# Interleaving the projection slabs of the second block's attention, with a buffer of its own for the compressed weights

## The chip, the cores and the metric

The kernel runs on one core of a Trainium2 chip. The metric is the device time of one execution in microseconds (us), as the median of several runs. The engines are TensorE (PE, matrix products), VectorE (DVE), ScalarE (ACT), GpSimd (POOL) and SyncE (SP, which here only issues the loads). Each engine works through its own list of instructions in order and waits on semaphores that the others raise.

## The reference, cut to what matters

Two layers of a first block come first; the change touches none of them. The second block then computes, for 512 tokens of width 1024:

```python
hn = rms_norm(h, attn_pre_norm)
proj = hn @ w_in                                   # one product, cut into the parts below
(q_n, k_c, v_c, k_s, v_s, k_w, v_w, g_n, q_w, k_sw, v_sw) = jnp.split(proj, IN_SPLITS, axis=-1)
qn = rope(q_n); k_c, k_s, k_w = rope(k_c), rope(k_s), rope(k_w)
ckv = compress(stack([k_c, v_c]), cmp_pos, cmp_w1, cmp_w2)    # gelu(blocks @ w1) @ w2, for keys and for values
o_cmp, p_cmp = compressed_attention(qn, ckv[0], ckv[1], t)
o_slc = selected_attention(qn, k_s, v_s, idx, t)              # 8 blocks of 64, 16 are chosen: all of them
o_win = banded_attention(qn, k_w, v_w, 512, None)
gates = sigmoid(g_n)
o_nsa = gates[0] * o_cmp + gates[1] * o_slc + gates[2] * o_win
o_swa = banded_attention(rope(q_w), rope(k_sw), v_sw, 128, swa_sinks)
mixed = concat(rms_norm(o_nsa), rms_norm(o_swa)) @ w_out
```

after which come a residual, a feed-forward part and the output.

## The kernel before, in words

All weights come in **slabs** of 128 x 1024 floats. SP loads a slab into one of four slots (`raw`), ACT copies it to `w_hi` (line 1099, function `split`), DVE subtracts to get the remainder `w_lo` (line 1510), and PE multiplies: each product is three matmuls, high by high, high by low and low by high (`mm3`, lines 534 to 536). `w_hi` and `w_lo` have two halves (`SPL = 2`), used in turn: slab n may be split when PE is through with slab n - 2 (semaphore `slab_used`), and a slot can be loaded again when DVE has split its slab (`lo_ready`).

The attention part of the second block has 25 slabs, which before come in three runs:

- 13 **t slabs** (`T_ORDER`, lines 792 to 812): the values to be compressed, then the keys kc, ks, kw, kx, then four slabs of queries qn and four of sliding queries qx. PE makes 24 matmuls of 512 columns for each. ACT copies the bank out (line 1372) and copies it once more with halves swapped (line 1374, four instructions); DVE rotates (function `rope`, lines 1825 to 1840: two products and one sum, or four half sums for ks, kw, kx).
- 4 **v slabs** (lines 815 to 824): values and gates, 24 matmuls of 408 columns each. ACT then copies the values out (`v2`, lines 1394 and 1395) and takes exponentials of the gates.
- 8 **c slabs** (function `cmp_hidden`): the weights `cmp_w1`, four for keys and four for values, each only 12 matmuls of 256 columns. Their other operand are the blocks `xe_hi`, `xe_lo`, which DVE builds out of the rotated keys and the raw values (functions `blocks` and `blocks_low`) with one ACT copy between (line 1388).

Then a chain of small steps makes the compressed branch: a gelu (line 1402), two transposes (842), copies (1406), the second weights (856, 861), copies (1408, 1410), 64 score matmuls of 31 columns (875), mask, maximum and difference on DVE (1883 to 1891, `cmp_front`), exponentials on ACT (1414), sums and coefficients on DVE (1899 to 1910, `cmp_back`), 32 transposes (886) and copies of them (1432). The attention proper goes over a list of units (`UNITS`), as a pipeline: scores (903 and 909), maximum (1943), exponential (1426), scaling (1959), transposes (922), copies (1444), products with the values (943). The first two units' scores stand before the 32 transposes, the others behind.

The order on each engine is written out by hand: each of the blocks for SP, PE, ACT and DVE has its own loop over the slabs, and the step that belongs to slab i is put into the loop by a condition on i.

## Time and profile before

| | |
|---|---|
| time, median of 3 runs | 1905.05 us (1902.78 to 1906.3) |
| the profiled execution: span, first to last instruction | 1903.6 us |
| PE busy | 1829.9 us, 96% of the span |
| DVE, ACT, POOL busy | 1333.0, 973.8, 190.6 us |
| mean granted clock of PE | 0.985 |
| slabs of the second block's attention part, in that execution | 1199.4 to 1312 us |
| small steps of the compressed branch | 1312 to 1336.8 us |

The page gives no time of the profiled execution other than its span; what lies around the span is not in it. The span stands 1.45 us under the median of the runs and inside their range. The times in the rows below count from the span's start. A granted clock of 1.00 is the upper of TensorE's two levels (2.4 GHz), 0.50 the lower (1.2 GHz).

### The profile page before, as it was taken

What the parts mean: (1) busy time and instruction counts of PE and PEld (TensorE: products, weight loads), DVE (VectorE), ACT (ScalarE), POOL (GpSimd) and SP (SyncE); (2) the same over time, 40 slices, a digit from 0 to 9 for tenths busy, and PEclk for the clock granted to TensorE, in tenths of its full rate; (3) what the DMA queues carried; (4) which work ended last, traced back from release to release, by engine and by line L of the source; (5) the groups of instructions that cost most, each with busy time, mean ns of one, the idle gap of its engine ahead of it and who ended that gap; (6) DMA issues with size and microseconds to landing.
All of it is one profiled execution on the core that took longest, in us unless ns stands there. A gap on an engine that the chain in (4) does not pass through costs nothing.

```text
span 1903.6 us, 27030 instructions
## 1 busy us (share of the span) xinstructions
PE 1829.9 (96%) x8975; PEld 1456.3 (77%) x8975; DVE 1333.0 (70%) x1885; ACT 973.8 (51%) x1550; POOL 190.6 (10%) x135
## 2 busy tenths in 40 slices
PE   6999999999999999999999999997998999999998
PEld 5775778888888875678888888886656678888887
DVE  6989677777655899767777655694666477777544
ACT  5569654444433468764444443674655554444322
POOL 0100120000133100120000033100012300000111
PEclk9999999999999999999999999997999999999999
DMA  6220233333234330133333233434000223332332
GB/s 172 68 77 1 67 93 95 99 99 93 77 98 117 84 81 12 34 94 95 99 99 94 76 100 97 107 85 132 1 1 2 88 71 94 99 99 84 86 98 75
DMA packets 285095, 154.46 MB, mean 81 GB/s; under 512 B 16949, under 2 KB 283095, under 8 KB 285015
## 3 DMA queue, kind: packets, MB, share of 16 engines
q1 hardware_dynamic: 284596, 153.26, 27.9%
q8 instruction: 45, 0.74, 0.2%
q14 instruction: 35, 0.29, 0.0%
q10 hardware_dynamic: 419, 0.17, 0.0%
HBM read 151.31 MB, written 2.10 MB: 81 GB/s over the span
## 4 chain that ended last, share of the span: by engine, by line
PE 78%; DVE 10%; issue 6%; ACT 5%; DMA 0%; DVEq 0%; SPq 0%; ACTq 0%
PE bank L534 24%; PE bank L536 23%; PE bank L535 23%; DVE cacc L1647 3%; PE bank L903 1%; DVE w_lo L1510 1%; PE bank L943 1%; DVE nmax L1714 1%; PE bank L922 1%; ACT w_hi L1099 1%; DVE pr L1959 1%; DVE nmax L1943 1%; PE bank L1018 0%; DMA x_in<-in_x 0%; PE bank L683 0%
## 5 line engine op out<-in xcount | busy, mean ns | idle before, releaser
L1099 ACT ACTIVATE w_hi<-raw 128x1024 fp32r<-128x1024 f32 (+1 forms) x337 | 336.2, 1004 | 511.9 <-PE bank L536 507.4
L1510 DVE TENSOR_TENSOR w_lo<-raw,w_hi 128x1024 fp32r<-128x1024 f32 (+1 forms) x337 | 404.0, 1204 | 256.2 <-ACT w_hi L1099 255.3
L534 PE MATMUL bank<-h_hi,w_hi 128*128 128x512 f32 x1448 | 569.6, 393 | 10.9 <-DVE w_lo L1510 10.7
L535 PE MATMUL bank<-h_lo,w_hi 128*128 128x512 f32 x1448 | 564.5, 390 | 0.0
L536 PE MATMUL bank<-h_hi,w_lo 128*128 128x512 f32 x1448 | 564.4, 390 | 0.0
L534 PEld LDWEIGHTS bank<-h_hi,w_hi 128*128 128x128 f32 x1448 | 272.5, 188 | 75.2 <-issue 11.9
L535 PEld LDWEIGHTS bank<-h_lo,w_hi 128*128 128x128 f32 x1448 | 272.3, 188 | 58.3 <-issue 2.2
L536 PEld LDWEIGHTS bank<-h_hi,w_lo 128*128 128x128 f32 x1448 | 272.4, 188 | 56.6
L534 PE MATMUL bank<-a_hi,w_hi 128*128 128x512 f32 x528 | 206.1, 390 | 0.0
L536 PE MATMUL bank<-a_hi,w_lo 128*128 128x512 f32 x528 | 205.5, 389 | 0.0
L535 PE MATMUL bank<-a_lo,w_hi 128*128 128x512 f32 x528 | 205.4, 389 | 0.0
L1647 DVE SCALAR_TENSOR_TENSOR cacc<-u_pad,lc,cacc 128x512 f32<-128x512 f32 x240 | 179.5, 793 | 1.6
L1595 DVE TENSOR_TENSOR zr<-bank,rstd 128x512 f32<-128x512 f32 x132 | 90.8, 688 | 80.5 <-PE bank L536 68.4
L1601 DVE SCALAR_TENSOR_TENSOR tz<-zr,lc,tz 128x511 f32<-128x511 f32 x176 | 131.9, 750 | 19.9 <-DVE tz L1601 6.8
L1168 ACT ACTIVATE a_hi<-tz 128x512 f32 (+1 forms) x66 | 41.8, 633 | 160.6 <-DVE tz L1609 160.6
L536 PEld LDWEIGHTS bank<-a_hi,w_lo 128*128 128x128 f32 x528 | 99.1, 188 | 20.8
L534 PEld LDWEIGHTS bank<-a_hi,w_hi 128*128 128x128 f32 x528 | 99.1, 188 | 20.5
L535 PEld LDWEIGHTS bank<-a_lo,w_hi 128*128 128x128 f32 x528 | 99.1, 188 | 20.2
L2027 POOL TENSOR_TENSOR sq<-x 128x512 f32 (+1 forms) x16 | 29.3, 1832 | 636.6 <-DVE x L1790 636.6
L1611 DVE TENSOR_TENSOR a_lo<-tz,a_hi 128x512 f32 x66 | 45.7, 693 | 61.5 <-ACT a_hi L1168 61.5
L1164 ACT ACTIVATE tz<-zr,lc 128x512 f32<-128x512 f32 x88 | 71.1, 808 | 31.4 <-DVE zr L1595 31.4
L1601 DVE SCALAR_TENSOR_TENSOR tz<-zr,cols,tz 128x510 f32<-128x510 f32 x88 | 65.9, 749 | 9.4 <-DVE tz L1601 1.7
(313 smaller groups left out, 2217.9 us busy)
## 6 DMA issues: line engine op xcount, KB each, us to landing
raw<-in_w_up SPq DMA_DIRECT2D x132, 512.0 KB, 3.7
raw<-in_w_in SPq DMA_DIRECT2D x39, 512.0 KB, 3.9
raw<-in_w_down SPq DMA_DIRECT2D x48, 384.0 KB, 3.1
raw<-in_w_down SPq DMA_DIRECT2D x48, 320.0 KB, 2.9
raw<-in_w_o SPq DMA_DIRECT2D x16, 512.0 KB, 3.4
raw<-in_cmp_w SPq DMA_DIRECT2D x8, 512.0 KB, 4.0
raw<-in_w_out SPq DMA_DIRECT2D x8, 512.0 KB, 4.3
raw<-in_w_uq SPq DMA_DIRECT2D x8, 288.0 KB, 2.9
```

Source lines behind the costliest of these rows:

```text
L534: mm(o, wh, mh, start=start, stop=False)
L535: mm(o, wh, ml, start=False, stop=False)
L536: return mm(o, wl, mh, start=False, stop=stop)
L1099: last = A_(dst(w_hi), src(raw), ACT.Copy)
L1164: A_(tz[:, s, :], zr[:, s % 2, :], ACT.Identity, bias=c_b(ch), scale=c_w1(ch)).then_inc(z1_done.sem, 1)
L1168: A_(a_hi[:, bass.ds(i * 2 + j, 1), :], tz[:, 2 * j + 1:2 * j + 2, :], ACT.Copy).then_inc(ah_done.sem, 1)
L1510: last = v.tensor_tensor(dst(w_lo), src(raw), dst(w_hi).bitcast(f32), ALU.subtract)
L1595: v.tensor_tensor(zr[:, s % 2, :], bank[s][:, :], rstd[:, 0, :], ALU.mult).then_inc(zr_done.sem, 1)
L1601: ins = v.scalar_tensor_tensor(tz[:, s, a:b], zr[:, s % 2, a + sh:b + sh], tap(n, ch), tz[:, s, a:b], ALU.mult, ALU.add)
L1611: v.tensor_tensor(a_lo[:, bass.ds(i * 2 + j, 1), :], tz[:, 2 * j + 1:2 * j + 2, :], a_hi[:, bass.ds(i * 2 + j, 1), :].bitcast(f32), ALU.su ...
L1647: ins = v.scalar_tensor_tensor(cacc[:, c, :], src, wc, cacc[:, c, :], ALU.mult, ALU.add)
L2027: link(p.tensor_tensor(sq[:, :], chunk, chunk, ALU.mult))
```

## The change

A table `SEQ2` sets one order of the 25 slabs for all engines: v slabs go between the first t slabs, the c slabs go singly between other slabs, and the sliding queries come last. The c slabs get buffers of their own (`cw_hi`, `cw_lo`); the other slabs go on using `w_hi` and `w_lo` in turn (`ring2`), and a slab waits for the slab before it in the same buffer (`before2`). The banks are dealt out anew (`T_BANK`, `VG_B`), `swapped` becomes two buffers. The steps of the compressed branch are put between the slabs: the gelu and transposes for keys behind the fourth c slab and t6, the scores behind the last c slab, the mask and exponentials at t10, the transposes at t11. The last rotation (the fourth qx) moves into the attention pipeline's third round on DVE.

```diff
+SEQ2 = [("t", 0), ("t", 1), ("v", 0), ("t", 2), ("v", 1), ("t", 3), ("v", 2), ("c", 0), ("t", 4), ("c", 1), ("v", 3),
+        ("c", 2), ("t", 5), ("c", 3), ("t", 6), ("c", 4), ("t", 7), ("c", 5), ("t", 8), ("c", 6), ("t", 9), ("c", 7),
+        ("t", 10), ("t", 11), ("t", 12)]
+T_BANK = (0, 1, 0, 1, 0, 1, 2, 3, 0, 1, 0, 2, 3)
+def ring2(n):
+    return sum(kind != "c" for kind, _ in SEQ2[:n]) % SPL
+def before2(n):
+    same = [m for m in range(n) if (SEQ2[m][0] == "c") == (SEQ2[n][0] == "c") and (SEQ2[n][0] == "c" or ring2(m) == ring2(n))]
+    return same[-1] if same else 1
...
 # SP
+            for p, (kind, i) in enumerate(SEQ2):
+                if p == 6:
+                    sp.wait_ge(x_done.sem, x_done.at(DEPTH, 0))
...
 # PE
+            def turned_slab(p, i):
+                for j in banked_before(i):
+                    pe.wait_ge(rc_done.sem, j + 1)
+                    pe.wait_ge(sw_done.sem, j)
...
+            for p, (kind, i) in enumerate(SEQ2):
+                slab_ready(G2, p)
...
+                if (kind, i) == ("t", 3):
+                    root_columns()
+                if (kind, i) == ("t", 6):
+                    cmp_turn(0)
+                if (kind, i) == ("t", 7):
+                    cmp_keys()
+                if (kind, i) == ("c", 7):
+                    cmp_scores()
+                if (kind, i) == ("t", 10):
+                    cmp_turn(1)
+                if (kind, i) == ("t", 11):
+                    cmp_values()
+                    for n in range(2 * NT):
+                        cmp_turned(n)
...
+                if u == 1:
+                    pe.wait_ge(sw_done.sem, 12)
...
-                if s == 1:
-                    for n in range(2 * NT):
-                        cmp_turned(n)
 # ACT, split
+                if isinstance(g, int) and g == G2 and SPL <= n0 < S2_O:
...
+                    act.wait_ge(slab_used.sem, G2 * RAW + before2(n0) + 1)
+                    A_(halves2(n0)[0], raw[:, n0 % RAW, :], ACT.Copy).then_inc(hi_ready.sem, 1)
+                    return
 # ACT, loop
+            for p, (kind, i) in enumerate(SEQ2):
...
+                split(N, G2, p + SPL)
+                if (kind, i) == ("t", 10):
+                    log_exp_table()
+                    for e in range(2):
+                        act.wait_ge(cs_sub.sem, e + 1)
+                        A_(cs[:, e, :, :], cs[:, e, :, :], ACT.Exp).then_inc(cs_exp.sem, 1)
+                act.wait_ge(slab_used.sem, G2 * RAW + p + 1)
+                if kind == "t":
+                    copied(i)
...
+                if (kind, i) == ("t", 3):
+                    act.wait_ge(rcol_mm.sem, 1)
...
+                    blocks_high(0)
+                if (kind, i) == ("v", 3):
+                    values_out()
+                if (kind, i) == ("c", 2):
+                    blocks_high(1)
...
+                if (kind, i) == ("t", 10):
+                    turned_out(1)
 # DVE, loop
+            for p, (kind, i) in enumerate(SEQ2):
...
+                if p + SPL < S2_O:
+                    split(G2, p + SPL)
...
+                if p == 3:
+                    blocks(0)
+                if kind == "t" and i >= 3:
+                    rope(i - 2)
+                if (kind, i) == ("v", 2):
+                    blocks_low(0)
+                if (kind, i) == ("v", 3):
+                    blocks(1)
+                if (kind, i) == ("t", 5):
+                    blocks_low(1)
...
+                if (kind, i) == ("t", 10):
+                    cmp_front()
+                if (kind, i) == ("t", 11):
+                    cmp_back()
...
+                if s == 2:
+                    rope(len(ROPED) - 1)
```

What the tables do to the order of instructions is seen at three places. Line numbers in the lists of the change are those of the changed kernel; lines 1164 and 1171 there are ACT's slab copy (1099 before), 1606 DVE's remainder (1510 before).

**ACT, at the exponentials of the compressed scores (`cs`).** Before:

```order
L1406 ACTIVATE hid<-bank 128x62
L1408 ACTIVATE kcT<-bank 128x62 [waits kv_mm]
L1410 ACTIVATE vcn<-bank 31x128 [waits kv_mm]
L1104 ACT_TABLE_LOAD
L1414 ACTIVATE cs<-cs 128x496 [waits cs_sub] x2
L1426 ACTIVATE pr_91,rsum<-bank,nmax 128x128 [waits nm_done] x4
L1432 ACTIVATE ct_all<-bank 31x4x128 [waits ct_mm] x8
```

With the change:

```order
L1164 ACTIVATE w_hi<-raw 128x1024 [waits slab_used,raw_ready0]
L1176 ACT_TABLE_LOAD
L1480 ACTIVATE cs<-cs 128x496 [waits cs_sub] x2
L1438 ACTIVATE tz<-bank 128x512 [waits rope_done,slab_used]
L1440 ACTIVATE swapped_84<-bank 32x512 x4
L1465 ACTIVATE hid<-bank 128x62 [waits hid_t]
L1465 ACTIVATE hid<-bank 128x62
L1171 ACTIVATE w_hi<-raw 128x1024 [waits slab_used,raw_ready1]
L1438 ACTIVATE tz<-bank 128x512 [waits rope_done,slab_used]
L1440 ACTIVATE swapped_83<-bank 32x512 x4
L1510 ACTIVATE vcn<-bank 31x128 [waits kv_mm]
L1514 ACTIVATE ct_all<-bank 31x4x128 [waits ct_mm] x8
```

The exponentials stood behind all slab work; now they stand between the split of the last t slab (t12) and the copies of the banks of t10 and t11, and the copies of the values' hidden part (`hid`) stand behind them.

**DVE, at the mask and the sums of the compressed scores.** Before:

```order
L1510 TENSOR_TENSOR w_lo<-raw,w_hi 128x1024 [waits hi_ready,rope_done]
L1510 TENSOR_TENSOR w_lo<-raw,w_hi 128x1024 [waits hi_ready] x11
L1915 TENSOR_SCALAR gates<-gates 128x96 [waits gate_exp]
L1916 RECIPROCAL gates<-gates 128x96 [waits dve_link]
L1883 TENSOR_TENSOR cs<-bank,const 128x496 [waits cs_mm] x2
```

With the change:

```order
L1606 TENSOR_TENSOR w_lo<-raw,w_hi 128x1024 [waits hi_ready] x2
L1927 TENSOR_TENSOR tz<-tz,const 128x512 [waits sw_done]
L1928 TENSOR_TENSOR tz<-swapped_83,const 128x512
L1937 TENSOR_TENSOR qx<-tz 128x512 [waits dve_link]
L1946 TENSOR_TENSOR cs<-bank,const 128x496 [waits cs_mm,rope_done]
```

and, behind the rest of `cmp_front` and one scaling of x:

```order
L2017 SCALAR_TENSOR_TENSOR x<-x,cols,rstd 128x512
L1927 TENSOR_TENSOR tz<-tz,const 128x512 [waits sw_done]
L1928 TENSOR_TENSOR tz<-swapped_84,const 128x512
L1937 TENSOR_TENSOR qx<-tz 128x512 [waits dve_link]
L1962 TENSOR_REDUCE csum<-cs 128x16 [waits cs_exp,rope_done]
```

The mask addition now stands behind the remainder of t12 and a rotation, and the sums behind one more rotation, which waits for the swapped copy of t10.

**DVE, at the first blocks' remainder `xe_lo`, which the first c slab waits for.** With the change:

```order
L1606 TENSOR_TENSOR w_lo<-raw,w_hi 128x1024 [waits hi_ready]
L1606 TENSOR_TENSOR cw_lo<-raw,cw_hi 128x1024 [waits hi_ready]
L1927 TENSOR_TENSOR tz<-tz,const 128x512 [waits sw_done]
L1928 TENSOR_TENSOR tz<-swapped_84,const 128x512
L1937 TENSOR_TENSOR k_ks<-tz 64x512 [waits dve_link]
L1937 TENSOR_TENSOR k_ks<-tz 64x512 x3
L1606 TENSOR_TENSOR w_lo<-raw,w_hi 128x1024 [waits hi_ready,rope_done]
L1919 TENSOR_TENSOR xe_lo<-xe,xe_hi 128x1088 [waits xe_h]
L1606 TENSOR_TENSOR cw_lo<-raw,cw_hi 128x1024 [waits hi_ready]
```

Before, this step stood at the ninth t slab with four t slabs and all v slabs between it and the first c slab; now it stands at the last slab before that c slab.

## Rows read from the trace of the kernel before

**Rows 1.** Busy time by stage: stretch, its length, busy us (instructions) per engine, PE clock.

```profile
core 0: us, PE busy (x) PEld busy (x) DVE busy (x) ACT busy (x) POOL busy (x), PEclk, DMA share, GB/s
1273.50:1292.40 18.90, 18.30 (x98) 17.89 (x97) 11.57 (x14) 8.43 (x11) 0.00 (x0) 1.00 0.36 114
1292.40:1312.00 19.60, 14.42 (x98) 13.15 (x97) 8.77 (x8) 13.08 (x22) 0.00 (x0) 0.91 0.57 180
1312.00:1336.80 24.80, 17.45 (x125) 13.94 (x124) 11.60 (x26) 9.93 (x26) 0.00 (x0) 0.59 0.22 66
```

**Rows 2.** Waits from 1199 to 1341 us: total us, times, longest.

```profile
PE bank L534 <- DVE w_lo L1510: 6.3, 6, 2.6
```

**Rows 3.** PE in order of time, c slabs: start, us, instruction, [idle before <- releaser].

```profile
1299.34 0.39 PE L534 MATMUL bank<-w_hi,xe_hi 128*128 128x256 f32 x1 [2.57 <-DVE w_lo L1510]
...
1306.18 0.39 PE L534 MATMUL bank<-w_hi,xe_hi 128*128 128x256 f32 x1 [0.58 <-DVE w_lo L1510]
```

**Rows 4.** PE in order of time, small steps and first units.

```profile
1313.56 0.33 PE L842 MATMUL bank<-const,hidc 62*128 62x62 f32 x2 [1.23 <-ACT hidc L1402]
...
1314.42 1.06 PE L861 MATMUL bank<-w2v,hid 128*31 128x64 f32 x8
1315.84 7.04 PE L875 MATMUL bank<-kcT,qn 64*128 64x31 f32 x64 [0.36 <-ACT vcn L1410]
...
1330.02 1.92 PE L886 MATMUL bank<-const,cs 128*31 128x128 f32 x8 [5.17 <-DVE cs L1910]
...
1335.80 1.07 PE L886 MATMUL bank<-const,cs 128*31 128x128 f32 x8 [0.32 <-ACT ct_all L1432]
1336.81 0.70 PE L903 MATMUL bank<-k_ks,qn 64*128 64x256 f32 x4
...
1339.31 0.44 PE L922 MATMUL bank<-const,pr 128*128 128x128 f32 x2 [0.50 <-DVE pr L1959]
```

**Rows 5.** Busy time and PE clock in three stretches of the small steps.

```profile
1315.00:1322.60 7.60, 7.24 (x69) 7.00 (x67) 0.41 (x1) 1.55 (x2) 0.00 (x0) 0.50 0.40 128
...
1325.00:1330.00 5.00, 0.00 (x0) 0.00 (x0) 4.83 (x13) 1.90 (x6) 0.00 (x0) 0.50 0.00 0
...
1335.00:1337.00 2.00, 1.68 (x15) 1.11 (x14) 0.00 (x0) 1.63 (x4) 0.00 (x0) 1.00 0.00 0
```

**Rows 6.** ACT in order of time.

```profile
1222.95 1.06 ACT L1099 ACTIVATE w_hi<-raw 128x1024 fp32r<-128x1024 f32 x1 [1.33 <-PE bank L536]
1224.04 0.60 ACT L1372 ACTIVATE tz<-bank 128x512 f32<-128x512 f32 x1
1224.66 2.40 ACT L1374 ACTIVATE swapped<-bank 32x512 f32<-32x512 f32 x4
1228.39 1.06 ACT L1099 ACTIVATE w_hi<-raw 128x1024 fp32r<-128x1024 f32 x1 [1.33 <-PE bank L536]
...
1256.49 1.12 ACT L1388 ACTIVATE xe_hi<-xe 128x1088 fp32r<-128x1088 f32 x1
...
1326.18 1.20 ACT L1414 ACTIVATE cs<-cs 128x496 f32<-128x496 f32 x2 [9.09 <-DVE cs L1891]
```

**Rows 7.** DVE in order of time.

```profile
1224.11 1.23 DVE L1510 TENSOR_TENSOR w_lo<-raw,w_hi 128x1024 fp32r<-128x1024 f32 x1 [0.30 <-ACT w_hi L1099]
...
1232.59 2.78 DVE L1838 TENSOR_TENSOR k_kw<-tz 64x512 f32<-64x512 f32 x4
...
1244.76 0.69 DVE L1838 TENSOR_TENSOR qn<-tz 128x512 f32<-128x512 f32 x1
...
1257.71 1.29 DVE L1820 TENSOR_TENSOR xe_lo<-xe,xe_hi 128x1088 fp32r<-128x1088 f32 x1 [0.51 <-ACT xe_hi L1388]
...
1322.91 1.25 DVE L1883 TENSOR_TENSOR cs<-bank,const 128x496 f32<-128x496 f32 x2 [7.50 <-PE bank L875]
...
1327.05 1.24 DVE L1899 TENSOR_REDUCE csum<-cs 128x16 f32<-128x496 f32 x2
```

**Rows 8.** Loads on SP's queue, from the page: times issued, KB, us to landing.

```profile
raw<-in_cmp_w SPq DMA_DIRECT2D x8, 512.0 KB, 4.0
```

More of the change, by code:

```diff
@@ L278, in build @@
         STAT = bank[7]
-        VG_B = bank[4], bank[5], bank[1], bank[2]
+        VG_B = bank[4], bank[5], bank[2], bank[3]
         C_B, CT_B = (bank[4], bank[5]), (bank[6], bank[7])
@@ L807, in _, with value_slab @@
                 last.then_inc(slab_used.sem, 1)
-                if i == 5:
-                    pe.wait_ge(rr_done.sem, 1)
-                    for t in range(NT):
-                        last = mm(bank[6][:, t:t + 1], zr[0:1, 0, t * P:(t + 1) * P], ones[0:1, 0:1], start=True, stop=True)
-                    last.then_inc(rcol_mm.sem, 1)
-            pe.wait_ge(sw_done.sem, len(ROPED) - 2)
-            for i in range(KD // VG_K):
-                slab_ready(G2, S2_V + i)
-                w = parts(S2_V + i, VG_K, VG)
+            def value_slab(p, i):
+                w = parts2(p, VG_K, VG)
                 for t in range(NT):
@@ L849, in _ @@
-            pe.wait_ge(gate_exp.sem, NT)
-            cmp_turn(0)
-            cmp_turn(1)
-            pe.wait_ge(w2_ready, 48)
-            pe.wait_ge(rope_done.sem, len(ROPED))
-            pe.wait_ge(hid_done.sem, 2)
-            for m in range(2):
-                last = mm(bank[4][:, 0:2 * NC], w2k[:, m, :], hid[:, m, :], start=m == 0, stop=m == 1)
-            last.then_inc(kv_mm.sem, 1)
-            pe.wait_ge(hid_done.sem, 4)
-            for v in range(KV2):
-                for m in range(2):
-                    last = mm(bank[5][0:NC, v * HD2:(v + 1) * HD2], hid[:, 2 + m, v * NC:(v + 1) * NC], w2v[:, m, :],
-                              start=m == 0, stop=m == 1)
@@ L863, in _, with cmp_keys, cmp_values @@
-            last.then_inc(kv_mm.sem, 1)
+            def cmp_keys():
+                pe.wait_ge(w2_ready, 48)
+                pe.wait_ge(hid_done.sem, 2)
+                for m in range(2):
+                    last = mm(bank[4][:, 0:2 * NC], w2k[:, m, :], hid[:, m, :], start=m == 0, stop=m == 1)
+                last.then_inc(kv_mm.sem, 1)
+            def cmp_values():
+                pe.wait_ge(hid_done.sem, 4)
+                pe.wait_ge(sw_done.sem, 9)
+                for v in range(KV2):
+                    for m in range(2):
+                        last = mm(bank[1][0:NC, v * HD2:(v + 1) * HD2], hid[:, 2 + m, v * NC:(v + 1) * NC], w2v[:, m, :],
+                                  start=m == 0, stop=m == 1)
+                last.then_inc(kv_mm.sem, 1)
@@ new lines, in _ @@
+                if (kind, i) == ("t", 11):
+                    act.wait_ge(kv_mm.sem, 2)
+                    A_(vcn[0:NC, :], bank[1][0:NC, 0:KV2 * HD2], ACT.Copy).then_inc(kv_done.sem, 1)
+                    for n in range(2 * NT):
+                        e, t = divmod(n, NT)
+                        act.wait_ge(ct_mm.sem, n + 1)
+                        A_(ct_all[0:NC, :, t, e, :], CT_B[n % 2][0:NC, :].rearrange("p (c n) -> p c n", c=PAIRS),
+                           ACT.Copy).then_inc(ct_done.sem, 1)
@@ L1919, in evict @@
+            for n0 in range(S2_O - SPL, S2_O):
+                split(G2, n0 + SPL)
             def evict(i):
```

295 lines of the change are left out of this document (150 added, 145 removed).

## The prediction

> **What bounds the kernel now.** I read the busy time by stage first, then the waits, then PE's own order of time, and last ACT and DVE at the places that PE waits for. In the t and v slabs PE is the bound: in the v stage it is busy 18.30 of 18.90 us at full clock [rows 1]. In the c stage it is busy only 14.42 of 19.60 us at a mean clock of 0.91, and in the small steps 17.45 of 24.80 us at 0.59 [rows 1]. PE's work is the same before and after the change, and so is everything up to the first slab and after the first few attention units. So I count what PE loses between these two points, as waits and as clock, in both versions; the difference is the change of the time.
>
> **What PE loses now.** Waits: 6.3 us for slabs that DVE has not split yet [rows 2], most of it between c slabs, as the 2.57 and 0.58 us [rows 3]; 1.23 us for the gelu, 0.36 for the copies behind it, 5.17 for mask, exponentials and coefficients, 0.32 twice for copies of transposes, 0.50 at the first units [rows 4]: together 14.2 us. Clock: busy time times the missing share of the clock, 14.42 x 0.09 = 1.3 in the c stage and 17.45 x 0.41 = 7.2 in the small steps [rows 1]: 8.5 us. The sum is 22.7 us, which is also the most that any order of this work could gain.
>
> **What the change takes away.** The run of short c slabs goes, with its waits, and the steps of the compressed branch get slabs to run beside. If all of it were hidden, the 22.7 us would be gone. It is not, because each engine still takes its list in order, and some steps now stand behind others that are late.
>
> **The front, where a c slab waits for DVE.** The first c slab (c0) needs `xe_lo`. Its chain starts when PE ends t3: ACT copies the bank, 0.60 + 2.40 us, and the two small copies of the column roots (0.3, my estimate), then makes `xe_hi`, 1.12, then splits the second c slab, 1.06 [rows 6], because DVE's list has the remainder of that slab, 1.23, ahead of `xe_lo`, 1.29 [rows 7]. With three hand-offs of 0.1 (ACT's split ends at 1224.01, DVE's starts at 1224.11 [rows 6, 7]) that is 8.3 us. PE has beside it only v2, 18.30 / 4 = 4.6 [rows 1], and the column roots (1.0 us, estimated as eight matmuls like those of the small steps, which take 1.06 [rows 4]). So c0 waits some 2.7 us. The fifth c slab (c4) waits likewise. Behind the remainder of t6 DVE has a rotation of kx (two products of 0.69 and 2.78: 4.2), the values' `xe_lo` (1.29), two gate steps and one scaling of x (1.5 together, estimated from the 0.69 of one operation), and then the split of c4, 1.23 [rows 7]: 8.2 us; PE has t6, 5.44 (ACT's splits stand 5.44 apart, at 1222.95 and 1228.39 [rows 6]) and a transpose of 0.33 [rows 4]: 5.8. So c4 waits 2.4. I add 1.5 for c3, t6 and the score matmuls, where ACT's eight copies of the values and the last query rotation are a little late (two or three waits of the size of the 0.58 [rows 3]). Front: 6.6 us. It is at least 0, if ACT and DVE get ahead, and at most some 9.
>
> **The tail, where a chain goes through four lists.** At t10 ACT's list has: the split of t12, which waits for the end of t10 (the same half of `w_hi`); the exponentials, which wait for DVE's differences; then the copies of t10 and of the values' hidden part. DVE's list has the remainder of t12, a rotation, and only then mask, maximum and difference. So from the end of t10: split 1.06, remainder 1.23, rotation 3 x 0.69 = 2.1, mask to the first difference 3.3 (1322.91 to the exponentials at 1326.18), exponentials 1.20, copies 3.00, two small copies 0.5 (estimate), and some 0.1 each for six hand-offs: 13.0 us [rows 6, 7]. PE has t11 and one transpose beside it, 5.44 + 0.33 = 5.8. So PE stands still for **7.2 us** before the compressed values (line 861 of the kernel before). What is queued behind it on PE is everything, the transposes and t12 included. The next wait follows at once: DVE's rotation of t10's queries waits for the same copies, and the sums stand behind it: 2.1 + 3.0 (1327.05 to PE's first transpose at 1330.02 [rows 4, 7]) = 5.1, less the two small copies and the values' 1.06: some **3.5 us** before the transposes. These wait for their copies as before, 0.6. Behind them comes t12, 5.44, and the first unit; the second unit's bank was t12's, so it waits for ACT's split and copies, 1.06 + 3.00 + 0.3 = 4.4, less a first unit's scores of at most 0.9: **3.5 us**. Then the last rotation, 2.1, stands in DVE's list before the scaling that the first products wait for, on top of the 0.50 of before [rows 4]: 2.6, and I take 3.0, since the 32 transposes no longer cover the first pair's maximum and exponentials. Tail: 17.8 us.
>
> **The clock.** Before, the transposes behind the 5.17 us wait ran at 0.50 at first; the 32 of them took 1330.02 to 1336.81 with 0.6 of waits, 6.2, against 4 x 1.07 = 4.3 at the pace of the last eight [rows 4, 5]: 1.9 lost. They stand behind a longer gap now, so I take 1.9 again, 0.5 for the compressed values (half of 1.06), 1.3 for one of the two front gaps (the c stage's loss behind its 2.57 us gap [rows 1, 3]) and 0.7 for the second unit's start (half of what two units take). The 64 score matmuls took 7.04 us at 0.50 [rows 4, 5]; they follow a c slab now, and I take them at full clock, at no loss. Clock: 4.4 us; 0 at the least, and some 8 if every gap in front and t12 too are hit.
>
> The Trainium skill (TensorE: Matmul & The Clock Gate, section on HAM oscillation in real kernels) says that idle gaps between bursts of matmuls are what brings TensorE down to half its clock, and advises keeping bursts close together. By it the long gap of the new tail costs clock as well as time, and breaking up the run of c slabs saves clock in front; the trace agrees as to gaps, but it also has 7.24 busy us out of 7.60 at 0.50 [rows 5], which the advice alone would not give. What the rule would do if it held in the change's favour is the first rival.
>
> **Parts costed at nothing.** The loads: SP issues the same loads, the second weights of the compressed branch (three small loads) eleven slabs sooner; its wait ahead of them has been met by then. A load is issued four slabs ahead and lands in 4.0 us [rows 8]; between issue and use at least two slabs pass, one of them of 5.44, so it stays hidden; without that cover each late slab would cost up to 4.0. The bank waits of t slabs two positions apart are covered by the v and c slabs between. POOL has nothing here. ACT's and DVE's total work fits beside PE's and is unchanged but for where it stands.
>
> **The sum.** After: 6.6 + 17.8 + 4.4 = 28.8 us lost, before: 22.7. The change costs 6.1 us: 1903.6 + 6.1 = 1909.7 us for the profiled span. The median of the runs stands 1.45 above that span, so I forecast **1911 us**.
>
> **The rivals.** A measurement of this kernel can tell 0.2%, 3.8 us, from no change: 1901.2 to 1908.9 count as no difference.
> (1) The clock stays up. Then 28.8 - 4.4 = 24.4 against 22.7: 1.7 us slower, 1906.8, no difference. For it: the front's slabs are dense, and c slabs stand between long ones. Against it: the gap of 2.57 us before was followed by a stage at 0.91, and the tail's gap is longer [rows 1, 3].
> (2) DVE keeps pace in front. If `xe_hi` and the c slabs' splits get through before PE asks, the front's 6.6 and its 1.3 of clock go: 20.9, or 1.8 us faster, 1903.3, no difference. It decides from the point where c0 and c4 show no wait. Against it: the sums 8.3 against 5.6 and 8.2 against 5.8.
> (3) Faster: the exponentials are back before t10 ends. The score matmuls are done a whole t slab earlier; if DVE's mask came ahead of the remainder of t12, the chain would be over beside t10 and t11, the 7.2 and 3.5 would go and with them the 1.9 and 0.5 of clock: 15.7 lost, 7.0 us faster, **1898**. Against it: DVE's list has the remainder first, and that waits for ACT's split, which waits for the end of t10.
> That the change doesn't move what it says is no case: the order of the lists shows it.
>
> **How the numbers follow.** The forecast's case has 0.70, (1) 0.12, (2) 0.10, (3) 0.08. The forecast's own case runs from 1907 to 1918: 28.8 with the front at 4 and the clock at 3, up to the front at 9 and the clock at 8. I let the range reach down over (1) and (2), to 1903, which leaves out (3) and some of the edges. Faster is (3) and the lower edge of (2), 0.10; no difference is (1), most of (2) and the lower edge of the forecast's case, 0.26; slower is the rest, 0.64.
>
> **What would show it.** In the profile after: PE idle of about 7 us ahead of the compressed values' matmuls, released by ACT's `hid` copies; a second idle of 3 to 4 us ahead of the transposes; a third at the second unit, released by ACT's swapped copy of t12; two waits of 2 to 3 us at c0 and c4, released by DVE; ACT's exponentials idle for some 5 us for DVE's differences; half clock around the transposes. The prediction is wrong if the compressed values' matmuls follow t11 without a wait, or if PE's lost time in front is over 10 us, when the slab supply would be the bound.

## The result: 11 to 16 us slower, and more than forecast

| | before | with the change |
|---|---|---|
| median of the runs | 1903.91 us (1902.71 to 1906.3, 4 runs) | 1919.7 us (1918.1 to 1921.15, 4 runs) |
| ratio, 95% interval | | 1.0075 (1.0062 to 1.0089) |
| the same on a second occasion | 1906.87 us (10 runs) | 1917.78 us (4 runs), ratio 1.0060 (1.0044 to 1.0077) |
| profiled execution: time, span | span 1903.6 us | 1919.27 us, span 1917.2 us |
| mean granted clock | 0.985 | 0.980 |

The change costs 11 to 16 us. The forecast was 6 us, with a range up to 1918: the sign was right, the size too small. The first median lies 1.7 us above the range, that of the second occasion inside it: on which side of the range's end it falls is partly chance. The account below goes by the profile.

The waits of PE in the profile of the changed kernel, from 1199 to 1365 us (total us, times, longest):

```profile
PE bank L899 <- ACT hid L1465: 6.2, 1, 6.2
PE bank L926 <- DVE cs L1973: 3.6, 1, 3.6
PE bank L973 <- ACT swapped L1440: 3.5, 1, 3.5
PE bank L575 <- issue: 2.3, 1, 2.3
PE bank L575 <- DVE cw_lo L1606: 2.0, 1, 2.0
PE bank L992 <- DVE pr L2062: 1.6, 1, 1.6
```

The run of c slabs with its 6.3 us of waits [rows 2] is gone. In its place stand the waits that the prediction named: 6.24 us before the values' product (line 899), 3.60 before the transposes (926), 3.47 before the second unit (973), 2.25 and 1.97 at c0 and c4 (575). For c0 the profile names no releaser ("issue"), but DVE's `xe_lo`, which c0 needs, ended at 1239.09 and c0 began at 1239.19 (first line below). How the longest wait comes about is seen in DVE's and in ACT's order of time (start, us, instruction, idle before and what ended it):

```profile
1237.81 1.28 DVE L1919 TENSOR_TENSOR xe_lo<-xe,xe_hi 128x1088 fp32r<-128x1088 f32 x1
...
1307.44 1.22 DVE L1606 TENSOR_TENSOR w_lo<-raw,w_hi 128x1024 fp32r<-128x1024 f32 x1 [10.09 <-ACT w_hi L1164]
...
1310.63 1.26 DVE L1946 TENSOR_TENSOR cs<-bank,const 128x496 f32<-128x496 f32 x2
```

```profile
1313.91 1.20 ACT L1480 ACTIVATE cs<-cs 128x496 f32<-128x496 f32 x2 [5.20 <-DVE cs L1954]
1315.02 0.58 ACT L1438 ACTIVATE tz<-bank 128x512 f32<-128x512 f32 x1
```

The scores were finished at 1297.8. DVE idled 10.09 us for the high half of t12 (line 1606), and only then, behind a rotation, came to the mask (1946); ACT idled 5.20 us for DVE. So far the prediction holds. What it has wrong is in the busy time by stage of the changed kernel (columns as in rows 1; the last stretch, inside the one before it, runs from the scores of the third unit to those of the seventh):

```profile
1239.00:1293.40 54.40, 51.86 (x270) 44.91 (x270) 40.76 (x57) 36.50 (x60) 0.00 (x0) 0.97 0.47 136
1293.40:1312.20 18.80, 18.50 (x114) 15.13 (x114) 6.76 (x10) 5.37 (x7) 0.00 (x0) 0.82 0.26 84
1312.20:1335.00 22.80, 12.65 (x65) 9.18 (x65) 12.69 (x22) 12.91 (x24) 0.00 (x0) 0.78 0.07 24
1335.00:1360.40 25.40, 20.30 (x117) 10.73 (x116) 15.43 (x46) 14.50 (x43) 0.00 (x0) 0.66 0.07 22
1340.20:1354.40 14.20, 12.56 (x57) 6.17 (x56) 9.85 (x33) 6.34 (x24) 0.00 (x0) 0.50 0.02 5
```

The clock is down behind the scores (0.82) and in the first units (0.66, for 14 us 0.50). The third to the eighth unit in the kernel before:

```profile
1336.80:1350.10 13.30, 12.80 (x105) 7.11 (x104) 10.58 (x34) 9.65 (x31) 0.00 (x0) 1.00 0.01 2
```

and two lines of PE's order of time in the changed kernel, the second unit behind its wait and the fifth, whose 64x384 products took 0.92 us before:

```profile
1339.17 0.80 PE L973 MATMUL bank<-k_kw,qn 64*128 64x128 f32 x4 [3.47 <-ACT swapped L1440]
...
1346.61 1.65 PE L973 MATMUL bank<-k_ks,qn 64*128 64x384 f32 x4
```

From the third unit's start to the ninth's the kernel before took 13.3 us (1336.81 to 1350.15), the changed kernel 20.2 (1340.23 to 1360.43), the same matmuls. At the third unit the changed kernel is 3.4 us behind, at the ninth 10.3. That is the place to explain. These times count from the span's start. The first slab of this part starts anywhere from 1198.0 to 1200.9 us in the profiles below, though all kernels are the same up to there (1199.43 before, 1198.89 with the change); counted from that slab the changed kernel is 4.0 us behind at the third unit and 10.8 at the ninth. Where a text below says "from the first slab", it counts so.

Theories for the runs below: **A**, the waits are the cost, and the clock is a small term as the prediction has it; **B**, the lower clock behind these gaps was undersized; **C**, the cost sits in the front, in the interleaved c slabs. A and B don't exclude each other.

### The profile page after: what moved, and what is told of

It reads as the page before. It is cut to its first block, busy times and chain, and to the rows that moved or that the text cites. A ratio compares the mean times of both kernels' runs of the same rounds, so it can differ in the third digit from the quotient of the medians.

```text
span 1917.2 us, 27037 instructions
## 1 busy us (share of the span) xinstructions
PE 1837.7 (96%) x8975; PEld 1460.4 (76%) x8975; DVE 1333.1 (70%) x1885; ACT 973.0 (51%) x1550; POOL 191.2 (10%) x135
## 4 chain that ended last, share of the span: by engine, by line
PE 79%; DVE 9%; issue 6%; ACT 5%; DMA 0%; DVEq 0%; SPq 0%; ACTq 0%
PE bank L575 24%; PE bank L576 23%; PE bank L577 23%; DVE cacc L1746 3%; PE bank L973 2%; PE bank L1013 1%; PE bank L992 1%; DVE nmax L1813 1%; DVE w_lo L1609 1%; DVE pr L2062 1%; DVE nmax L2046 1%; ACT w_hi L1171 1%; PE bank L724 0%; DMA x_in<-in_x 0%; ACT swapped L1440 0%
## 5 line engine op out<-in xcount | busy, mean ns | idle before, releaser
L575 PE MATMUL bank<-h_hi,w_hi 128*128 128x512 f32 x1448 | 571.3, 395 | 10.9 <-DVE w_lo L1609 10.2
L1171 ACT ACTIVATE w_hi<-raw 128x1024 fp32r<-128x1024 f32 (+3 forms) x314 | 312.0, 1000 | 488.2 <-PE bank L577 483.7
L1609 DVE TENSOR_TENSOR w_lo<-raw,w_hi 128x1024 fp32r<-128x1024 f32 (+3 forms) x314 | 376.0, 1203 | 237.7 <-ACT w_hi L1171 237.1
L575 PEld LDWEIGHTS bank<-h_hi,w_hi 128*128 128x128 f32 x1448 | 273.3, 189 | 74.9 <-issue 10.6
L1527 ACT ACTIVATE pr<-bank,nmax 128x257 f32<-128x257 f32 (+5 forms) x96 | 47.3, 498 | 54.2 <-DVE nmax L2046 49.1
```

What stands on the lines that cost most here:

```text
L575: mm(o, wh, mh, start=start, stop=False)
L1171: last = A_(dst(w_hi), src(raw), ACT.Copy)
L1527: A_(pr2[:, s % 3, e, 0:n], S2_B[s % 2][e][:, c0:c0 + n], ACT.Exp, bias=nmax[:, st:st + 1], accum_out=rsum[:, st:st + 1]).then_inc(e_done. ...
L1609: last = v.tensor_tensor(dst(w_lo), src(raw), dst(w_hi).bitcast(f32), ALU.subtract)
```

## Experiments

Each run's own kernel before ran beside it on the same chip; "against before" is the difference of those two medians. Kernels of one group ran together, save where said (`fill_tail` ran with group 2, the two other runs of group 1 with group 6).

**1. The gaps filled.** Extra matmuls on PE that nobody reads stand in its waits: 24, 14 and 13 in `fill_tail`, the 13 alone in `fill_units`. `after_again` is the changed kernel itself, beside `fill_units`.

```diff
+            def fill(to, n):
+                for i in range(n):
+                    mm(to[:, :], ones_r[:, :], h_hi[:, i % KD, :], start=i == 0, stop=i == n - 1)
...
+                    fill(bank[6], 24)
                     cmp_values()
+                    fill(bank[6], 14)
                     for n in range(2 * NT):
...
+                if s == 1:
+                    fill(bank[4], 13)
                 if s < len(UNITS):
                     scores2(s)
```

> The changed kernel with 51 extra TensorE products (128x512, 0.227 us each in its rows) into a bank that nobody reads, put where its TensorE waits: 24 (5.4 us) into the wait of 6.24 us before the values' second product, 14 (3.2 us) into the 3.60 us before the transposes, 13 (3.0 us) between the first and the second unit of the attention (3.47 us). Every wait stays as long as it was, only the idle time is used. Theory A (the waits themselves are the cost, the clock is a small term, as the prediction had it): same time within 1 us, 1918 to 1921. Theory B (the lower clock that follows these gaps was undersized: 0.78 over 12.65 busy us and 0.66 over 20.30 busy us make 2.8 + 6.9 us): the granted clock from 1312 to 1360 us comes near 1.00 and the time falls by 5 to 9 us, to 1910 to 1914.

> The changed kernel itself once more, beside the others on one chip and with a second profile: 1917 to 1921, 13 to 16 us above the kernel before. In its profile the ninth unit of the attention starts within 1 us of 1360.4, as the order of the program sets it; what lies behind that (556.8 us to the end in the first profile, 553.4 in the kernel before, the same instructions) comes out between 553 and 558: if it is near 554, the 3 us there are chance, if near 557, they belong to the change.

> The changed kernel with the third of the three fills of the run fill_tail alone: 13 extra products (3.0 us) between the first and the second unit of the attention, into a bank that nobody reads. Theory B1 (the lower clock that costs is the one behind the gap between the first units, 17 us of units at half speed): 5 to 6.5 us faster than the changed kernel, as fill_tail was. Theory B2 (it begins with the gaps of 6.24 and 3.60 us further ahead, and the units only go on with it): under 2 us faster.

Measured: `fill_tail` 1913.38 us, 7.8 against before, where the changed kernel has 11 to 16 (granted clock 1.00 and 0.93 in the stretches that had 0.78 and 0.66); `after_again` 1917.78, 10.9 against before (13 to 16 expected); `fill_units` 1914.51, 7.6. The third fill alone does what the three do. The four runs of `fill_units` went from 1912.9 to 1918.4 us, those of `after_again` from 1916.6 to 1918.2: the medians alone don't separate the two, and the reading rests on the profiles. PE's order of time in `fill_units` and the busy time from its third to its eighth unit:

```profile
1334.33 3.29 PE L905 MATMUL bank<-h_hi,ones_r 128*128 128x512 f32 x13
1338.00 0.49 PE L977 MATMUL bank<-k_kw,qn 64*128 64x128 f32 x4 [0.38 <-ACT swapped L1446]
...
1344.26 0.92 PE L977 MATMUL bank<-k_ks,qn 64*128 64x384 f32 x4
```

```profile
1338.80:1354.30 15.50, 12.98 (x104) 7.15 (x104) 13.56 (x43) 9.74 (x33) 0.00 (x0) 1.00 0.03 11
```

The wait for ACT ends where it ended before, 4.2 us behind the first unit's start; PE worked in it, and the units behind run at 1.00, where the first 14 us of the changed kernel's had 0.50 (64x384 in 0.92 us, not 1.65). They take 15.5 us in place of 20.2. Theory B (form B1): 4.7 us of the change's cost is the clock behind the 3.47 us gap between the first two units. In the medians it is 3.3 us beside `after_again`, less than the 5 to 6.5 expected. In `fill_tail` the units take 17.1 us: the third and fourth run at full speed, but behind a later wait of 2.22 us the fifth is at half (1.54 us). The second profile of the changed kernel agrees with the first (20.1 us for the units, 161.5 us from the first slab to the ninth unit in both); from the ninth unit to the end it took 556.1 us, the first 556.8: in the upper half of the range expected.

**2. The chain ahead of the splits.** `chain_early` moves the mask to the differences ahead of DVE's remainder of t12, the exponentials ahead of ACT's split of t12, the sums ahead of a rotation. `chain_query_first` also puts t12 ahead of the values' product and the transposes on PE.

```diff
 # DVE
+                if (kind, i) == ("t", 10):
+                    cmp_front()
                 if p + SPL < S2_O:
                     split(G2, p + SPL)
+                if (kind, i) == ("t", 11):
+                    cmp_back()
...
 # PE and ACT, chain_query_first alone
-                if (kind, i) == ("t", 11):
+                if (kind, i) == ("t", 12):
                     cmp_values()
```

> The changed kernel with the chain of the compressed scores moved ahead in two lists: VectorE does the mask, maximum and subtraction before it waits for the high half of the last query slab (it stood idle 10.1 us there), ScalarE does the table and the exponentials before that high half, and VectorE does the sums and coefficients before the rotation. TensorE's order stays. The 6.24 us before the values' product and the 3.60 us before the transposes should go; 0 to 1.6 us may come up behind ScalarE's copy of the eleventh query (3 us) between the second and the third transposes; the 3.47 us before the second unit stays. Theory A: 8.2 to 9.8 us faster than the changed kernel, 1909.5 to 1911. Theory B: beside that, 2 to 5 us of clock, 1904 to 1908. Theory C (the cost sits in the front, in the interleaved compressed slabs, and the tail only shifts): less than 4 us faster, 1915 or more.

> As the run chain_early, and TensorE's last query slab before the values' product and the transposes, so that these cover ScalarE's 3 us of copies of it. The 3.47 us before the second unit should go; about 1 us should come up before the third transposes (ScalarE's copies 3.0 us and two smaller ones, against 1.06 + 2.1 us of TensorE's work). Theory A: 2 to 3.5 us faster than chain_early, 1906 to 1909. Theory B: 3 to 7 us faster than it, since the attention's first units no longer run behind a gap, 1898 to 1904.

Measured: `chain_early` 1911.74 us, 6.2 against before. The 6.24 us are gone, of the 3.60 are left 1.5, and 1.8 came up at the copies of the transposes: 6.5 us less waiting, and the third unit starts 7.4 us earlier from the first slab. Its units still take 20.4 us, at 0.63, for the 3.47 us gap stayed. In the medians, each against its own before, the gain on the changed kernel is 9.6 us by its first occasion and 4.8 by its second; by the profile it is theory A for these two waits, and C falls. `chain_query_first` 1905.2 us, 0.4 below before and 6.5 faster than `chain_early`: B's gain of 3 to 7, not A's of 2 to 3.5. Its rows:

```profile
1324.62 1.08 PE L926 MATMUL bank<-const,cs 128*31 128x128 f32 x8 [3.55 <-ACT ct_all L1514]
...
1331.38 0.70 PE L973 MATMUL bank<-k_ks,qn 64*128 64x256 f32 x4 [0.53 <-ACT pr L1527]
...
1335.94 0.44 PE L992 MATMUL bank<-const,pr 128*128 128x128 f32 x2 [2.35 <-DVE pr L2062]
1336.31 0.69 PE L1013 MATMUL bank<-pt,v 128*64 128x128 f32 x4
1336.93 1.65 PE L973 MATMUL bank<-k_ks,qn 64*128 64x384 f32 x4
```

The wait didn't shrink to 1 us as I expected: as much as before, 3.55 us, now stands between the transposes, since ACT copies t12's bank first. From the first slab the third unit starts 3.3 us earlier than in `chain_early` (the 3.47 us ahead of the second unit are gone, as is the 1.5 us before the transposes), and the units take 16.9 us in place of 20.4. So about half of the gain comes from fewer waits ahead of the units, and half lies in the units, which ran at 0.90 in place of 0.63: here a wait of the same length cost less ahead of the transposes than ahead of the first units.

**3. The last query out of the way.** As `chain_early`, with t12 in bank 7, which the first units don't need; ACT copies it after the sixth unit. The copies of t11 move behind those of the transposes, and the values' product behind the transposes.

```diff
-T_BANK = (0, 1, 0, 1, 0, 1, 2, 3, 0, 1, 0, 2, 3)
+T_BANK = (0, 1, 0, 1, 0, 1, 2, 3, 0, 1, 0, 2, 7)
...
 # ACT, attention loop; DVE's rotation of it moves from s == 2 to s == 8
+                if s == 5:
+                    copied(12)
```

> As the run chain_early, and the last query slab in a bank of its own (bank 7) that the first two units don't need: ScalarE copies the slab after the sixth unit, VectorE rotates it after the eighth (it is first used by the 17th unit), and the copy of the slab before it stands behind the transposes' copies. No wait of TensorE between the tenth query slab and the second unit should be over 1 us. Theory A: 3.5 to 5 us faster than chain_early, 1904.5 to 1907.5. Theory B: 5 to 9 us faster than it, 1896 to 1902, and below the kernel before (1903.9).

Measured (beside group 2): 1904.14 us, 1.5 below before (ratio 0.9992, 0.9981 to 1.0002): 7.6 us faster than `chain_early`, inside B's gain of 5 to 9, though not as low as B's 1902, since `chain_early` had come out at the upper end. Up to the third unit two waits over 1 us remain in the tail, 2.19 before the transposes (where none was expected) and 2.29 at the third unit, and the units take 18.8 us.

**4. A gap made on purpose.** On top of `last_query_later` PE waits ahead of the first unit for seven operations of POOL; then the same with 30 and with 41 extra matmuls in that wait (the last on another occasion).

```diff
 # POOL
+            for n in range(6):
+                link(p.tensor_tensor(sq[:, :], one, one, ALU.mult))
+            p.tensor_tensor(sq[:, :], one, one, ALU.mult).then_inc(gap_done, 1)
 # PE, first unit
+                    fill(bank[4], 30)
+                    pe.wait_ge(gap_done, 1)
```

> As the run last_query_later, with a wait of TensorE before the attention's first unit, made by seven steps of GpSimd that start when the last query slab is done (about 1.2 us each, 8 to 9 us in all; GpSimd does nothing else there). Theory A: slower than last_query_later by the wait less what the small waits behind it had (about 2 us), 6 to 8 us. Theory B: by the wait and 3 to 6 us of lower clock in the first units, 10 to 14 us.

> As the run gap_idle, with 30 extra products of TensorE (6.8 us) in that wait, into a bank that nobody reads. The wait's end doesn't move. Theory A: the same time as gap_idle within 1.5 us. Theory B: 4 to 7 us faster than gap_idle, since the first units run at the higher clock; 6 to 8 us slower than last_query_later.

> As gap_idle, with 41 extra products in the 9.82 us of that wait (9.8 us at the 0.239 us each that the 30 of gap_filled took), in place of the 30 that left its last 2.77 us open; into a bank that nobody reads. If the gap right ahead of the units is what lowers the clock: the products of the third to the sixth unit (64x256 and 64x384) run at 0.70 and 0.92 us, not 1.22 and 1.65, and the ninth unit starts 14 to 16 us behind the third, not 18.5; 3 to 5 us faster than gap_idle and gap_filled. If the small units lower it by themselves: half speed again, and the same 18 us.

Measured: `gap_idle` 1913.24 us, 9.1 against before; `gap_filled` 1914.93, 10.8; `gap_filled_whole` 1912.53, 7.8. `gap_idle` lies 10.6 us above `last_query_later`, each against its own before, which is the low end of B's 10 to 14; but the units of `last_query_later` were partly at half speed already, and in the profiles `gap_idle` is only 8.1 us behind it at the ninth unit, counted from the first slab. So this pair doesn't tell A from B. In `gap_idle` the units right behind the gap ran at half speed at once:

```profile
1336.64 0.80 PE L978 MATMUL bank<-k_ks,qn 64*128 64x128 f32 x4 [9.82 <-issue]
...
1338.94 1.22 PE L978 MATMUL bank<-k_ks,qn 64*128 64x256 f32 x4
```

The first fill was too short, as PE's order of time in `gap_filled` shows:

```profile
1326.33 7.16 PE L908 MATMUL bank<-h_hi,ones_r 128*128 128x512 f32 x30
1336.26 0.49 PE L983 MATMUL bank<-k_ks,qn 64*128 64x128 f32 x4 [2.77 <-POOL sq L2233]
1336.90 0.49 PE L983 MATMUL bank<-k_kw,qn 64*128 64x128 f32 x4
1338.20 1.23 PE L983 MATMUL bank<-k_ks,qn 64*128 64x256 f32 x4 [0.59 <-ACT pr L1540]
```

and in `gap_filled_whole`:

```profile
1326.56 9.73 PE L908 MATMUL bank<-h_hi,ones_r 128*128 128x512 f32 x41
1336.51 0.49 PE L983 MATMUL bank<-k_ks,qn 64*128 64x128 f32 x4 [0.23 <-POOL sq L2233]
1337.15 0.49 PE L983 MATMUL bank<-k_kw,qn 64*128 64x128 f32 x4
1338.45 0.70 PE L983 MATMUL bank<-k_ks,qn 64*128 64x256 f32 x4 [0.59 <-ACT pr L1540]
```

With 2.77 us left open the first two units still ran at full speed (0.49 us) and the third at half (1.23 us), with 0.23 us the third at full speed too (0.70); but for the length of the fill nothing in these rows differs. So here the gap right ahead lowers the clock, not the small units by themselves. The price is less than I expected. The busy time from the third to the eighth unit, `gap_idle` and `gap_filled_whole`:

```profile
1338.90:1357.30 18.40, 16.22 (x104) 8.79 (x104) 12.78 (x42) 13.98 (x41) 0.00 (x0) 0.78 0.01 1
1338.40:1355.00 16.60, 14.11 (x104) 7.90 (x104) 12.44 (x40) 13.87 (x41) 0.00 (x0) 0.93 0.01 1
```

That is 1.8 us where 3 to 5 were expected, since a later gap in these units, 2.1 us ahead of one unit's transposes, is followed by half speed in all three. The medians, 1.4 us apart against their own before, lie within each other's intervals and show nothing by themselves.

**5. Small products between large ones.** As `last_query_later`, with the scores spread over the eight steps of t10 and the transposes over those of t12; then also c0's and c4's waits taken away on DVE.

```diff
+                    if i == 10:
+                        cmp_scores(k)
+                    if i == 12:
+                        cmp_turned(k)
 # DVE, between_and_front alone
+                if (kind, i) == ("v", 2):
+                    blocks_low(0)
                 if p + SPL < S2_O:
                     split(G2, p + SPL)
+                if (kind, i) == ("c", 3):
+                    gate_sums()
```

> As the run last_query_later, and the small products put between the large ones: of the 64 score products (4.13 us in one piece in the profile of the changed kernel) eight behind every third of... each of the eight steps of the tenth query slab, and of the 64 transposes (8 us in one piece) eight behind each of the eight steps of the last query slab. No work is added or left out. Theory B (what follows a stretch of small products runs at the lower clock: the query slab behind the scores ran 0.63 us a product for 5.7 us, where 0.39 is usual): the granted clock of 1293 to 1312 us rises from 0.82 to 0.95 or more and that of the transposes' stretch too, 3 to 6 us faster than last_query_later, 1898 to 1901. Theory A (waits only): no wait is removed but up to 2 us before the transposes, 1902 to 1904.

> As the run between, and two steps of VectorE in the front in another order: the low half of the first blocks before the split that waits for ScalarE (2.25 us before the first compressed slab), the gates' sums and the final gain behind the split of the next compressed slab (1.97 us before the fifth). Both waits should shrink to under 1 us: 2.5 to 3.5 us faster than the run between by the waits, and some 1 us more by the clock (0.97 over 51.86 busy us in this stretch).

Measured (beside `gap_idle`): 1912.09 us, 8.0 against before, and 1906.9, 2.8. The first is a miss. The clock did rise: t10 and the scores took 11.5 us together at a granted clock of 1.00, where `last_query_later` took 12.5 at 0.73. But the order made new waits behind ACT, 3.0 us for the bank of t12 and 5.1 for the first exponentials. The second differs by the front alone: its two waits fell to 0.2 and 0.5 us (0.9 came up elsewhere), and from the first slab the first unit starts 3.6 us earlier.

**6. The versions that beat both.** `later_and_front` is `last_query_later` with the front of group 5. `later_front_sums` also puts the sums right behind the differences on DVE and the splits of the first two output slabs into the attention.

```diff
 # DVE
                 if (kind, i) == ("t", 10):
                     cmp_front()
+                    cmp_back()
...
-            for n0 in range(S2_O - SPL, S2_O):
-                split(G2, n0 + SPL)
...
+                if 6 <= s < 6 + SPL:
+                    split(G2, S2_O + s - 6)
```

> As the run last_query_later, with VectorE's two steps in the front in the other order (those of between_and_front: the low half of the blocks ahead of a split, the gates' sums and the final gain behind one), and the small products in one piece again. Theory A: 2.5 to 3.5 us faster than last_query_later by the two waits (2.25 and 1.97 us) alone. Theory B: 3 to 5. Either way below the kernel before, by 3.5 to 6 us. If it is not faster than last_query_later, the waits of the front were paid for elsewhere.

> As the run later_and_front, with VectorE's sums and coefficients right behind the exponentials (it idled 5.6 us there) and the splits of the first two slabs behind the attention moved into the attention (2.4 us of VectorE and 1.1 of ScalarE stood between the last query slab and the first unit's maximum). The 2.19 us before the transposes and most of the 2.29 us before the third unit should go: 3 to 5 us faster than later_and_front, 6 to 10 us faster than the kernel before.

Measured (beside `fill_units`): 1898.61 us, 8.3 below before, ratio 0.9956 (0.9942 to 0.9969); and 1895.37, 11.5 below before, ratio 0.9946 (0.9932 to 0.9961). Both gains are somewhat larger than expected (3.5 to 6 and 6 to 10). The second version is faster than both kernels. Its largest waits of PE up to 1420 us, and the attention's first units, in order of time:

```profile
PE bank L995 <- DVE pr L2078: 4.6, 6, 1.0
PE bank L995 <- ACT pt L1546: 2.1, 1, 2.1
PE bank L928 <- ACT ct_all L1518: 1.5, 3, 0.9
```

```profile
1318.59 0.49 PE L976 MATMUL bank<-k_ks,qn 64*128 64x128 f32 x4
...
1320.52 0.70 PE L976 MATMUL bank<-k_ks,qn 64*128 64x256 f32 x4 [0.59 <-ACT pr L1534]
...
1323.76 0.92 PE L976 MATMUL bank<-k_ks,qn 64*128 64x384 f32 x4
```

From the first slab the third unit starts 19.5 us earlier than in the changed kernel and 15.6 earlier than in the kernel before.

**7. What the change's own two parts are worth.** From `later_front_sums`: the c slabs back in the common buffers, or in two rows of four, or both. (The kernel before has one row of eight, behind all other slabs.)

```diff
 # common_ring
-            if SEQ2[n0][0] == "c":
-                return cw_hi[:, :], cw_lo[:, :]
 # slabs_in_a_row
+        ("t", 7), ("c", 0), ("c", 1), ("c", 2), ("c", 3), ("t", 8), ("c", 4), ("c", 5), ("c", 6), ("c", 7), ("t", 9),
```

> The run later_front_sums once more, as the measure for the other three on the same chip: 1893 to 1898, 8 to 12 us faster than the kernel before.

> As later_front_sums, with the compressed slabs' split halves in the two common buffers again, in the same order of slabs. The slab behind a compressed one can then be split only once the slab ahead of the compressed one is used: 1.06 us of ScalarE and 1.22 us of VectorE (2.3 us) against the 1.4 us that TensorE takes for a compressed slab, so about 0.9 us of wait at each of eight places, more where VectorE rotates first. If the own buffers carry the front: 7 to 12 us slower than later_front_sums. If the common ones had done (the splits run ahead enough): within 2 us.

> As later_front_sums, with the compressed slabs in two rows of four (behind the eighth and the ninth query or key slab) in place of one by one between others; their one own buffer stays. In a row each slab waits for the split of the one before it to be used: 1.4 us of TensorE, then 2.3 us of ScalarE and VectorE, some 2.4 us of wait at six places: 14 us slower than later_front_sums if the waits alone count, 16 to 20 with the lower clock behind gaps.

> As slabs_in_a_row_own, with the common buffers, as the kernel before had both: about 1 us of wait at six places (6.3 us in the kernel before), 6 to 9 us slower than later_front_sums, so 1 to 5 us faster than the kernel before, which is then what the repaired tail and front are worth without the change's two parts.

Measured: `later_front_sums_again` 1896.71 us (8.3 below before); `common_ring` 1911.22, 14.5 slower than it; `slabs_in_a_row_own` 1919.19, 22.5 slower; `slabs_in_a_row` 1909.84, 13.1 slower. All three cost more than expected. The slabs' waits in `common_ring`, with the one before the scores:

```profile
PE bank L572 <- DVE w_lo L1614: 5.8, 8, 1.1
PE bank L914 <- DVE qn L1945: 3.1, 1, 3.1
```

in `slabs_in_a_row_own`:

```profile
PE bank L575 <- DVE cw_lo L1616: 14.8, 6, 2.5
PE bank L917 <- DVE qn L1947: 4.1, 1, 4.1
```

in `slabs_in_a_row`:

```profile
PE bank L572 <- DVE w_lo L1613: 8.5, 6, 2.5
PE bank L914 <- DVE qn L1944: 4.1, 1, 4.1
```

What the expectations left out is the wait before the scores, 3.1 to 4.1 us, for a rotation that is late as well, and the clock behind it: in all three the 64 scores took 7.04 us, where `later_front_sums` took 3.97. Neither part is worth anything without the other (rows with one own buffer are the worst); together they are worth 13 us in these lists, and 8 to 12 us against the kernel before, whose lists were written for its own order. The last run is 4.8 us slower than before, not faster as I expected.

## Why the prediction was wrong in its size

Its sum against the trace of the changed kernel:

| term | forecast | measured |
|---|---|---|
| front: c0, c4, small ones | 6.6 | 2.25 + 1.97 + 0.26 + 0.28 = 4.8 |
| before the values' product | 7.2 | 6.24 |
| before and between the transposes | 3.5 + 0.6 | 3.60 + 0.33 |
| second unit | 3.5 | 3.47 |
| last rotation ahead of a scaling | 3.0 | 1.64 |
| clock | 4.4 | 51.86 x 0.03 + 18.50 x 0.18 + 12.65 x 0.22 + 20.30 x 0.34 = 14.6 |
| sum | 28.8 | 34.6 |

34.6 less the 22.7 of before is 11.9; at the ninth unit the kernel is 10.8 us behind, counted from the first slab. Of the 1.1 us between, 0.9 is counted twice: from the third to the ninth unit the changed kernel took 6.9 us longer in all, and 1.1 of that is the longer wait (1.64 us for 0.50), so that with the second unit the clock took 6.0 there, not 6.9.

- **The waits** were right: 20.0 us of 24.4, each at its place, and with its releaser, the exponentials' 5.2 us for DVE included (at c0 the profile names none; the end of `xe_lo` and group 5 show DVE). One step of c0's chain is another than named: the split ahead of `xe_lo` is that of t4, not of the second c slab, with the same 1.06 us. The 4.4 us that the waits were put too high hid part of what the clock was put too low: had they been exact, the forecast would have been further off.
- **The step that failed is "Clock: 4.4 us"**, against 14.6 by the mean clock. In it, "0.7 for the second unit's start (half of what two units take)" stands against 6.0 to 6.9 in the units: the gap of 3.47 us didn't cost one unit's start but half speed for 14 us, and `fill_units` gave 4.7 of it back (20.2 to 15.5 us). And the scores "at full clock, at no loss" nearly ran so (4.13 us, 7.04 before), but the slab behind them did not: 3.3 us for both. The two other items were near: 1.6 and 2.8 us, forecast 1.3 and 2.4.
- **The upper bound of the clock**, 8 "if every gap in front and t12 too are hit", missed the units altogether. That moved the range's end too low. (With front 9 and clock 8 the prediction's own sum gives 1917, not 1918.)
- **What was costed at nothing**, the loads and the bank waits of the t slabs, cost nothing: no wait of the list names them.
- **Rival (1), the clock stays up**, had it the wrong way round. **Rival (3)** named the right cure: with the mask ahead of the remainder the 6.24 us went. Alone it wasn't enough, for 1.5 and 1.8 us of waits around the transposes, the second unit's gap and its clock stayed; with the last query moved, the front and the sums it was (1895 us).
- The span is 13.6 us longer: 10.8 from the first slab to the ninth unit, 3.3 behind it, and 0.5 less ahead. The 3.3 is no part of the change that I can name: see the last section. The 10.8 is what the second occasion's medians differ by (10.9).

The Trainium skill (TensorE: Matmul & The Clock Gate, section on HAM oscillation in real kernels) ascribes the half clock to idle gaps between bursts of matmuls. The pair of group 4 agrees (2.77 us open: 1.23 us for the third unit's product; 0.23 open: 0.70), though not every gap of such a length lowered it (last section). The slab behind the scores doesn't fall under it: PE was busy 18.50 of 18.80 us there, with no wait over 0.28 us.

## What to carry to other kernels

Price a new wait by what runs behind it, not by its length alone: look in the trace for short work right behind the gap, and count the half speed there as a term of its own. Before work is interleaved, walk each engine's list for steps that are ready early but stand behind one that waits: moving those (here the mask, sums, splits and copies) was worth more than the interleaving itself had cost (22 us by the medians of the second occasion, against 11 to 16). And test two parts of a change apart and together: here neither the order nor the buffers pay alone.

## What the runs showed of the hardware that I had not expected

The clock can fall behind work with hardly a gap. In the changed kernel the scores, behind 0.28 us of idle, ran at nearly full speed (4.13 us, 7.04 before), and the slab behind them at half for 5.7 us:

```profile
1293.68 4.13 PE L915 MATMUL bank<-kcT,qn 64*128 64x31 f32 x64 [0.28 <-DVE qn L1937]
1297.74 0.79 PE L575 MATMUL bank<-h_hi,w_hi 128*128 128x512 f32 x1
1298.33 0.63 PE L576 MATMUL bank<-h_lo,w_hi 128*128 128x512 f32 x1
...
1304.05 0.39 PE L575 MATMUL bank<-h_hi,w_hi 128*128 128x512 f32 x1
```

With the scores spread between t10's products (`between`) that stretch ran at 1.00; the 0.28 us went with it, so that the small products in one piece are the likely cause, not the shown one. In `fill_units`, the same up to there, the half speed behind the scores lasted only 2.7 us.

A gap doesn't always lower it either: behind 2.35 us in `chain_query_first` the fifth unit ran at half speed, behind 2.22 us at the same place in `fill_units` it did not, and behind the same 2.22 us in `fill_tail` it did. What decides there stays open; the price of one gap in one profile is no constant.

From the ninth unit to the end the instructions are all but the same in every version, and yet the profiles took 552.5 us (`later_and_front`) to 557.8 (`common_ring`), with 553.5 in the kernel before and 556.8 and 556.1 in the changed one. The kernel before itself ran from 1901.0 to 1910.6 us in the 29 runs beside group 2. A single profile of this kernel can't tell 3 us behind the ninth unit from chance; so the 3.3 us there stay unexplained.
